# Delta stage: the second weight split of each head moved from GpSimd's queue into VectorE's

## What is computed

```python
h = rmsnorm(x, norm_w[l])
proj = h @ w_in[l]
qkv = silu(short_conv(concat([q, k, v]), conv_w))      # 5 taps
q, k = l2norm(q), l2norm(k)                            # per head
T = inverse(eye + L)                                   # L from kb, k and the decays
def step(state, inp):                                  # over the chunks
    v_new = u_c - w_c @ state
    o = (q_c * exp(g_c)) @ state + qk_c @ v_new
    state = state * exp(g_last) + (k_c * exp(g_last - g_c)).T @ v_new
```

## Time and profile before

| what | us |
|---|---|
| runs | 3439.16 (median), 3438.78, 3450.72 |
| profiled execution, its own time | 3445.75 |
| its span, first to last instruction | 3443.9 |
| delta stage, heads 0 to 7, layer 1 | about 82 to 492 of the span |
| delta stage, heads 0 to 7, layer 2 | about 1090 to 1502 of the span |
| mean granted TensorE clock | 0.964 |

### The profile page before, as it was taken

The page is one execution under the profiler, slowest core; times in us unless marked ns, Lnnn a source line. Parts: engine busy times, 40 slices in busy tenths (PEclk is TensorE's granted clock), DMA queues, the critical chain, the costliest instruction groups (busy, mean ns, idle before and its releaser), DMA issues. The chain is left out here.

```text
span 3443.9 us, 56061 instructions
## 1 busy us (share of the span) xinstructions
PE 3170.1 (92%) x22464; PEld 2482.0 (72%) x22464; DVE 1689.8 (49%) x2498; ACT 1500.6 (44%) x2868; POOL 418.2 (12%) x276
## 2 busy tenths in 40 slices
PE   6999979999898999889997989988999999889998
PEld 4777767776676777767775856767888767678887
DVE  6666642566336666633665334453333354534343
ACT  4445442555324444433555334553333345533332
POOL 1434410000013444400000010001000000010000
PEclk9999999999899999999999989988999999989999
DMA  3111113222232111023221333103333231023332
GB/s 111 43 39 38 39 27 98 65 66 53 66 85 62 38 39 45 20 62 85 59 71 32 97 85 80 37 25 87 97 97 97 74 91 37 25 73 98 97 97 74
DMA packets 377883, 225.12 MB, mean 65 GB/s; under 512 B 25536, under 2 KB 357824, under 8 KB 377152
## 3 DMA queue, kind: packets, MB, share of 16 engines
q1 hardware_dynamic: 377664, 222.06, 23.8%
HBM read 214.68 MB, written 2.10 MB: 63 GB/s over the span
## 5 line engine op out<-in xcount | busy, mean ns | idle before, releaser
L300 PE MATMUL bank<-hT,ws 128*128 128x512 f32 x2144 | 915.9, 427 | 72.7 <-DVE hT L447 31.4
L304 PE MATMUL bank<-hT,ws 128*128 128x512 f32 x2144 | 848.6, 396 | 0.0
L303 PE MATMUL bank<-hT,ws 128*128 128x512 f32 x2144 | 847.3, 395 | 0.0
L300 PEld LDWEIGHTS bank<-hT,ws 128*128 128x128 f32 x2144 | 409.4, 191 | 230.2 <-issue 131.7
L267 DVE TENSOR_TENSOR ws<-raw,ws 128x2048 fp32r<-128x2048 f32 x172 | 395.2, 2298 | 262.7 <-ACT ws L261 255.2
L261 ACT ACTIVATE ws<-raw 128x2048 fp32r<-128x2048 f32 x184 | 351.7, 1911 | 335.8 <-PE bank L300 225.4
L304 PEld LDWEIGHTS bank<-hT,ws 128*128 128x128 f32 x2144 | 408.2, 190 | 91.3
L303 PEld LDWEIGHTS bank<-hT,ws 128*128 128x128 f32 x2144 | 410.7, 192 | 82.2 <-issue 13.4
L825 PE MATMUL bank<-uS,ws 128*128 128x512 f32 x512 | 201.8, 394 | 0.0
L829 PE MATMUL bank<-uS,ws 128*128 128x512 f32 x512 | 201.2, 393 | 0.0
L828 PE MATMUL bank<-uS,ws 128*128 128x512 f32 x512 | 200.3, 391 | 0.0
(11 more groups left out here) (354 smaller groups left out, 5026.2 us busy)
## 6 DMA issues: line engine op xcount, KB each, us to landing
raw<-in_w_in SPq DMA_DIRECT2D x196, 512.0 KB, 4.4
raw<-in_w_ff SPq DMA_DIRECT2D x128, 512.0 KB, 4.4
raw<-in_w_out SPq DMA_DIRECT2D x32, 512.0 KB, 5.1
raw<-in_w_pa SPq DMA_DIRECT2D x16, 512.0 KB, 5.3
raw<-in_w_pb SPq DMA_DIRECT2D x16, 512.0 KB, 5.4
raw<-in_w_in SPq DMA_DIRECT2D x16, 256.0 KB, 4.3
sq<-rq SPq DMA_DIRECT2D x48, 64.0 KB, 2.0
xT<-in_xT SPq DMA_DIRECT2D x1, 2048.0 KB, 7.6
```

The lines of the kernel that those rows point to most:

```text
L300: first = pe.matmul(out, hi, x[:, 0, k], start=(k == 0), stop=False)
L303: pe.matmul(out, hi, x[:, 1, k], start=False, stop=False)
L304: last = pe.matmul(out, lo, x[:, 0, k], start=False, stop=(k == KT - 1))
```

## The change

The low part of chunk 1 of head i+2 is no longer issued on GpSimd ahead of `norm_decay`, but on VectorE behind `norms`, in cores 0 to 5 of both layers, that is 12 times in all. What the instruction reads and writes and the semaphores it waits for and raises are the same.

```diff
@@ -1221,8 +1221,6 @@
                         if not first:
                             pool.wait_ge(x_taken, scratch_use("o", i) + 1)
                         beta_decay(i + 1, 1 - p, i)
-                        if ahead > 1:
-                            st.low(pool, i + 2, 1)
                         norm_decay(i + 1, 1 - p)
                 pool.memset(pad[:, :, :], 0.0).then_inc(zeroed, 1)
                 pool.memset(Xf[:, :, :, :], 0.0).then_inc(zeroed, 1)
@@ -1767,6 +1765,8 @@
                             drain(fill)
                         elif ahead:
                             norms(i + 1, 1 - p, i)
+                            if ahead > 1:
+                                st.low(dve, i + 2, 1)
                     if ahead > 1:
                         dve.wait_ge(r_ready, nth(i, 2 * (NS - 1), 2 * (NS - 2) + 1))
                         table(i + 2, p)
```

## The result

| | us |
|---|---|
| before, 15 runs | 3443.17 (median), 3438.18 to 3458.19 |
| after, 15 runs | 3463.28 (median), 3453.20 to 3472.81 |
| ratio | 1.0049, 95% interval 1.0034 to 1.0064 |
| profiled execution of after | 3456.80, span 3454.9 |

The change makes the kernel slower by about 16.9 us (0.49% of 3443.17; the interval is 11.7 to 22.0, and the two medians as they stand are 20.1 apart). The sign of the forecast was right; the size, +6.2 us, was 10.7 us short, and the median lies 5 us above the range.

What follows compares the result with a forecast made beforehand. It took PE's wait for `r` in step 3, on the chain into the next core, as deciding. Per core 2.29 + 0.03 - 1.80 = +0.52 us, twelve times +6.2 us, on 3439.16 gives 3445.4 us; range 3437 to 3458.

Steps and rivals of the forecast that it cites:

- The sign of the forecast: Whole kernel: slower, by 6.2 us or 0.18%; chance 0.72.
- The place: Step 3 of the delta stage's recurrence: PE waits for `r`, and a delay of `r` delays the whole next core.
- the order: After the norms, VectorE's split starts before GpSimd's `norm_decay`, which is then shown with about 3.2 us instead of 1.04.
- the stall: First norm instruction on VectorE stands still until GpSimd's split ends; the change takes away 1.80 us (1.97 to 0.17).
- The other order: After the norms, GpSimd's `norm_decay` gets in before VectorE's split: +1.53 us a core, +18.4 us, 3457.6; chance 0.13.
- The term of the sum: `r` of step 3, per core: 2.29 + 0.03 added, 1.80 taken away, +0.52 us; twelve times +6.2 us.
- Beside these the clock is a scatter of its own: Whole kernel: clock treated as scatter apart from the rivals; unchanged runs lie 12 us apart, 3438.78 to 3450.72.
- The base: Whole kernel: the median of the unchanged runs, 3439.16 us, to which +6.2 us was added.
- Absorbed: PE's fill products behind L1407 or the next core's idle time take up the 0.52 us: 0 us, 3439.2; chance 0.10.
- A gain: Freed stall worth more than the split costs, `r` at best 1.30 us earlier: down to -15.6 us, 3423.6; chance 0.05.

Runs made afterwards that it cites:

- the kernel with 2.20 us: Kernel before, with an idle VectorE maximum over 704 constants in front of `r`, 12 times; PE's wait 2.20 us; measured twice, 1.0033 and 1.0038.
- 1.80 us in longer heads: Changed kernel plus a useless 176-column product at the end of PE's work on a head; heads 54.13 and 55.73 us; 1.0029 against the kernel before.

## Why the prediction was wrong

- **The place, the order and the stall: right.** The stall goes from 1.97 to 0.17 in the 12 places (my "in all 16 places" overlooked the first one of each layer's stage, which takes 1.25 before and after), the split takes 2.29, VectorE comes before GpSimd, `norm_decay` is 3.08 (3.2 forecast). The other order, to which I gave 0.13, occurred in none of the 12 places. That the measured loss, 16.9 us, lies near the 18.4 us of that case is chance: a plain head has 53.81 us and not about 55.0, and the split kept its 2.29. What the Trainium skill says in SBUF — State Buffer, section "Who interferes with whom", fits these rows in the order and nearly in the size: the split was issued first and kept its 2.29 us, and GpSimd's instruction ended at 184.41 + 3.08 = 187.49, 0.90 us behind the split, where standing still until its end would have made 1.04.
- **The term of the sum: +0.39 instead of +0.52 for a head, 4.7 us instead of 6.2.** I let `r` wait for the split's shown end plus 0.03. It doesn't depend on the split, and starts 0.08 before that end (184.30 + 2.29 = 186.59, `r` at 186.51). This could have been read in the trace of before, where the instruction behind the split of the earlier trace rows, which ends at 62.72, doesn't wait for it either:

```profile
62.64 0.48 DVE L1645 TENSOR_SCALAR cb<-cb,cw 128x512 f32<-128x512 f32 x1
```

- **The step that failed** is the sentence "Beside these the clock is a scatter of its own". I priced PE's longer wait by its length at an unchanged clock and took the granted clock of 1.00 in the earlier trace rows as a given of this stage. At these 12 places it held with waits of 1.4 us and no longer with 1.8. The missing term is the number of slowed heads times 1.56 us, 6 x 1.56 = 9.4 us in both profiled executions of the change, more than my whole sum of 6.2. 4.7 + 9.4 = 14.1 us is 0.41%, inside the interval of 0.34% to 0.64%; the rest to 0.49% I haven't traced.
- **Why the single execution hid it.** The profiled spans differ by 3454.9 - 3443.9 = 11.0 us, less than the delta stage's 14.1 us, so the rest of that execution was some 3 us shorter, at nearly the same mean clock over the whole (0.964 and 0.965). The heads one by one showed what the whole span did not.
- **The base.** My forecast stood on the median of three runs, 3439.16; fifteen runs have 3443.17. 4 us of the distance of 17.9 us between forecast and median come from there.
- **The rivals.** "Absorbed" was wrong: the 0.39 is found in every plain head. "A gain" named the right bound, though not this change: with the split behind `r` a head gets 1.16 us shorter (forecast at best 1.30).

**What stays open:** why a wait of this size costs a stretch at one place and not at the next. The stretches don't begin at a fixed distance from the wait either: the earliest starts 0.2 us before the wait's end (in the kernel with 2.20 us), the latest 1.3 us behind it (in the changed one). How often they come: 6 and 6 of 12 heads in the changed kernel, 4 with the same wait and head where VectorE only idled, 5 and 5 with 2.20 us, 3 with 1.80 us in longer heads. In the changed kernel a plain and a slowed head add up to 53.81 + 55.37 = 109.2 us, and the stretches at 241.3 and 350.5 are as far apart. That this makes them return is argued and not shown; one or two executions of each are too little, and the kernel in which VectorE idled has fewer with the same lengths. The counts cover these 12 places alone. Stretches of half clock come elsewhere too, in the kernel before as well (its heads of core 6 have 1.00 and 0.93), and change in number: core 6 of layer 1 took 52.84 us at 0.87 where VectorE only idled, against 49.08 at 1.00 before, with no stretch behind the wait at its start.

## What to carry to other kernels

Where PE waits on a serial chain, ask not only which engine does a piece of work but on which side of the instruction that PE waits for it stands in the queue: the same split on the same engine is about 1.5 us a head dearer in front of `r` than behind it (53.81 against 52.28), before any effect of the clock. Price a wait of PE that grows past those the trace shows as a possible loss of clock as well, and look at the stage head by head, since a stretch of half clock cost 1.56 us where the wait itself had grown by 0.39. Take the whole time from many runs even so: with the wait of 2.20 us, what the heads lost was not all found in it. A wait that can't be removed is best filled with products that are due anyway; even useless ones won back most of the loss here.

## What the runs showed of the hardware

- A wait of PE of 1.80 us among dense work was followed, in 3 to 6 of 12 heads, by some 3.4 us at half clock (0.51 granted); waits of 1.42 us and of 0.72 us, in heads of about the same length, by none (12 places each). I had not expected a wait this short to do that.
- A longer wait (2.20 us) did not bring more of these stretches (5 of 12, twice), and 0.3 us of added work per head went along with fewer of them (3 of 12).
- A VectorE instruction on 4 values per partition stood still for 1.80 us behind GpSimd's long one, and in the other direction GpSimd's 1.04 us instruction was shown with 3.08 us behind VectorE's split: in these places whichever began first kept its usual length.
